# Constant-table matmuls ahead of the level scores, in the last recurrence of a two-block kernel

## The reference, cut to what matters

```
def step(state, inp):
    qi, ki, vi, gi = inp
    bcum = jnp.cumsum(gi, axis=2)
    o_inter = einsum('bhtk,bhkv->bhtv', qi * exp(bcum), state)
    rel = bcum[:, :, :, None, :] - bcum[:, :, None, :, :]
    decay = exp(where(incl, rel, -inf))
    scores = einsum('bhtk,bhsk,bhtsk->bhts', qi, ki, decay)
    o_intra = einsum('bhts,bhsv->bhtv', scores, vi)
    blast = bcum[:, :, -1:, :]
    state = state * exp(blast) + einsum('bhsk,bhsv->bhkv', ki * exp(blast - bcum), vi)
```

## Time and profile before

| | us |
|---|---|
| median of 3 runs | 3305.14 (3305.09 to 3307.75) |
| the profiled execution | 3311.11 |
| its span, first to last instruction | 3309.8 |
| TensorE matmuls busy | 3013.6 |
| VectorE busy | 1568.6 |
| ScalarE busy | 983.8 |
| GpSimd busy | 320.6 |
| mean granted TensorE clock (share of full speed) | 0.951 |

### The profile page before, as it was taken

The page is one execution under the profiler, slowest core; times in us unless marked ns, Lnnn a source line. Parts: engine busy times, 40 slices in busy tenths (PEclk is TensorE's granted clock), DMA queues, the critical chain, the costliest instruction groups (busy, mean ns, idle before and its releaser), DMA issues.

```text
span 3309.8 us, 44104 instructions
## 1 busy us (share of the span) xinstructions
PE 3013.6 (91%) x18434; PEld 2407.2 (73%) x18434; DVE 1568.6 (47%) x3075; ACT 983.8 (30%) x1912; POOL 320.6 (10%) x594
## 2 busy tenths in 40 slices
PE   7988889999999999888699999999999798699998
PEld 4657688889976666677557888888566587478886
DVE  3122544444443255776864424334625566655354
ACT  2011432223331155234233212211315344232222
POOL 0000000000000000543600000000100144200001
PEclk9999999999999999799799999999999799899999
DMA  5423241222122110222422121121011010222321
GB/s 180 152 93 128 83 123 42 55 60 75 58 96 102 51 32 1 80 71 79 148 101 83 45 77 64 51 77 64 39 45 33 16 33 20 90 90 77 115 83 71
DMA packets 227299, 246.62 MB, mean 75 GB/s; under 512 B 5552, under 2 KB 193052, under 8 KB 225564
## 3 DMA queue, kind: packets, MB, share of 16 engines
q1 hardware_dynamic: 227100, 243.79, 22.9%
HBM read 234.34 MB, written 9.44 MB: 74 GB/s over the span
## 4 chain that ended last, share of the span: by engine, by line
PE 56%; DVE 8%; ACT 4%; issue 1%; POOL 1%; DMA 1%; ACTq 0%; DVEq 0%; POOLq 0%
PE PS L1959 53%; PE PS L1963 2%; PE PS L2168 2%; ACT AR L174 1%; DVE AR L2687 1%; DVE AR L2678 1%; ACT L169 1%; DVE AR L2923 1%; POOL AR L2955 0%; DVE STAT L2859 0%; DVE EX L2910 0%; ACT EX L174 0%; DMA WR<-in_w_in 0%; DVE AC L2915 0%; ACT STAT L174 0%
## 5 line engine op out<-in xcount | busy, mean ns | idle before, releaser
L1959 PE MATMUL PS<-WR,HT 128*128 128x256 f32 (+2 forms) x2256 | 514.7, 387 | 11.0 <-ACT AR L174 5.4
L1959 PEld LDWEIGHTS PS<-WR,HT 128*128 128x128 f32 x2256 | 381.5, 199 | 120.2 <-issue 75.0
L1959 PE MATMUL PS<-HI,WC 128*128 128x512 f32 (+2 forms) x1600 | 428.2, 353 | 0.7 <-DVE WC L2904 0.7
L1959 PE MATMUL PS<-AR 128*64 128x64 f32 (+8 forms) x3756 | 320.6, 270 | 75.3 <-ACT AR L174 17.5
L1959 PE MATMUL PS<-HT,WR 128*128 128x256 f32 (+3 forms) x1136 | 357.3, 469 | 21.3 <-ACT EX L174 5.8
L174 ACT ACTIVATE AR<-PS 128x256 f32<-128x256 f32 (+3 forms) x389 | 166.1, 452 | 684.7 <-PE PS L1959 540.8
L1959 PEld LDWEIGHTS PS<-AR 128*64 128x64 f32 (+5 forms) x3756 | 276.8, 174 | 127.1 <-issue 48.7
L1959 PE MATMUL PS<-DW,DH 128*128 128x384 f32 (+1 forms) x1344 | 357.4, 348 | 0.9 <-DVE AR L2542 0.9
L1959 PEld LDWEIGHTS PS<-HI,WC 128*128 128x128 f32 x1600 | 284.1, 189 | 42.3 <-DVE WC L2904 1.1
L1959 PEld LDWEIGHTS PS<-HT,WR 128*128 128x128 f32 (+2 forms) x1136 | 214.6, 195 | 132.0 <-issue 91.3
L1959 PE MATMUL PS<-LO,WC 128*128 128x512 f32 (+2 forms) x800 | 282.6, 353 | 0.0
(11 more groups left out here) (297 smaller groups left out, 4142.3 us busy)
## 6 DMA issues: line engine op xcount, KB each, us to landing
WR<-in_w_ffn_in SPq DMA_DIRECT2D x40, 1024.0 KB, 7.6
WR<-in_w_in_b SPq DMA_DIRECT2D x51, 512.0 KB, 6.0
WR<-in_w_mod SPq DMA_DIRECT2D x12, 2048.0 KB, 8.1
WR<-in_w_mod SPq DMA_DIRECT2D x24, 1024.0 KB, 5.6
WR<-in_w_ffn_out SPq DMA_DIRECT2D x22, 1024.0 KB, 4.9
WR<-in_w_in SPq DMA_DIRECT2D x40, 512.0 KB, 4.1
WR<-in_w_out SPq DMA_DIRECT2D x8, 2048.0 KB, 9.3
WR<-in_w_in_a SPq DMA_DIRECT2D x8, 1024.0 KB, 5.2
```

The source lines that it names most:

```text
L1959: mm = lambda o, l, r, start, stop: e.o.matmul(o, l, r, start=start, stop=stop, skip_group_check=True)
```

## The change

Heads 2 and 3 of layer 1 get a mark `warm`. In `hl3` the wait for the unit's free banks moves ahead of the wait for its level weights, and for marked heads two matmuls stand between the two waits: the identity as stationary operand, the first 512 columns of the constant table as moving one, each into one bank of the unit's pair. The unit's own matmuls then start new sums in the same banks.

```
-        self.cum, ..., self.gneed = {}, {}, {}, False, False, False, None
+        self.warm, self.cum, ..., self.gneed = False, {}, {}, {}, False, False, False, None
...
+                H.warm = l == 1 and h > 1
...
             def hl3(n, H, i, d, L, until):
                 k, rev = H.dirs[d][0], H.dirs[d][2]
                 x3 = L["xb"][0:H.K, :].rearrange("p (l n) -> p l n", l=7)
+                e.wait_all(until)
+                for t in range(2 if H.warm else 0):
+                    mm(L["S"][:, t, :], ident, CON[:, 0:512], True, True)
                 e.wait_all(L["weighed"])
-                e.wait_all(until)
                 for t in range(2):
```

More of the change, by code:

```diff
@@ L247, in __init__ @@
         self.state, self.q_ready, self.steps, self.lv, self.am, self.slots = {}, {}, [], {}, {}, {}
-        self.cum, self.kt, self.dec, self.begun, self.multiplied, self.ended, self.gneed = {}, {}, {}, False, False, False, None
+        self.warm, self.cum, self.kt, self.dec, self.begun, self.multiplied, self.ended, self.gneed = False, {}, {}, {}, False, False, False, None
 def build(nc, A, out, dump=None):
```

## The result

The changed kernel takes 3321.95 us (median of 5 runs, 3317.20 to 3326.51) against 3305.86 for the kernel before on the same chip (3305.09 to 3307.75): ratio 1.0045, 95% interval 1.0034 to 1.0056. A second set of five runs gave 3318.77, ratio 1.0041 (1.0028 to 1.0053). So it is 12 to 16 us slower; 8.9 were forecast. Both sets are of five runs of one program, and their medians differ by 3.2 us.

A forecast was written before the change was run, and what follows sets the result against it. TensorE, busy 91% of the span, was taken as the bound wherever it does not idle. Terms 5.1 + 1.7 + 0.4 + 1.7 = 8.9 us on the 3305.14 median gave 3314.0, range 3308.5 to 3319.5.

The forecast's parts named there:

- head 2, units 0 to 2: Three pairs at full clock where TensorE does not idle: 3 x 1.71 = 5.1 us, all passed on.
- head 2, unit 3: Pair between transposes and unit: 0.7 of it at half clock, the rest and the unit at full clock; 1.7 us.
- head 3, unit 0 (units 1 and 2: 0): Unit 0's pair is mostly covered by 1.5 us free, leaving 0.4; units 1 and 2 are hidden in idle time.
- head 3, unit 3: Pair between a half-clock output and the unit whose end releases VectorE: 1.7 us if the clock runs as before.
- last output: Head 3's last output, at the recurrence's end: no change in the main case, half clock from 2856 on as before.
- the term for what lies behind the fence: After the recurrence: work starts from the shifted fence, so nothing takes the 8.9 us back; no further change counted.
- The slower rival of the prediction: Clock low more often, in heads 2 and 3: unit 3 of head 2 at 4.0, head 3 at 6.9; 3321, chance 0.07.
- my bounds of 0.5 and 4.0: Head 2's unit 3: 0.5 us with the clock up at once, 4.0 with the rise only behind the unit.
- the prediction's own sign of being wrong: Head 3: the prediction is wrong if the output before unit 3 runs at clock 1.00; 0.50 was expected.
- the clock stays up: Rival for head 3: it costs -0.3 instead of 2.1; 6.5 or 4.9 us in all, 3310 to 3311.6; chance 0.20.
- The rival's -0.7 for this piece: Head 3, unit 3: a full-clock output wins about 2.1, pays the pair, and VectorE is then the bound.
- My argument against the rival: Head 3: no pair stands in the gaps before 2844.94 and 2855.03; about 3 us idle remain ahead of the output.

The follow-up runs named there:

- swap_only: The two waits in the changed order with no matmul added, against the kernel before: 3305.83 us against 3306.54, ratio 0.9999.
- h3_gaps: Swapped waits and added pairs only before units 1 and 2 of head 3, against the kernel before: 3306.12 us against 3306.54, ratio 1.0001.
- tail: Pairs only before unit 3 of head 2 and units 0 and 3 of head 3, against the kernel before: 3309.97 us against 3305.35, ratio 1.0015.
- again: The changed kernel run and profiled once more, nothing altered, against the kernel before: 3318.77 us against 3306.54, ratio 1.0041.
- l0_first3: Three pairs before units 0 to 2 of head 2 in layer 0, none in layer 1, against the kernel before: 3313.21 us against 3305.35.
- after_fills: The changed kernel plus two constant-table matmuls for each of three idle times behind the recurrence: 3318.23 us, against 3305.35 for the kernel before.
- gapfill2: gapfill plus two matmuls in each of four later idle times, against the kernel before: 3299.48 us against 3306.00, ratio 0.9977.
- two_pairs: Pairs only before units 0 and 1 of head 2, against the kernel before: 3309.14 us against 3306.00, ratio 1.0011.
- one_pair: One pair only, before unit 0 of head 2, against the kernel before: 3312.90 us against 3306.00, ratio 1.0016.
- h2_first3: Pairs only before units 0 to 2 of head 2, against the kernel before: 3315.06 us against 3306.54, ratio 1.0026.
- gapfill: The kernel before with constant-table matmuls only in TensorE's idle times in heads 2 and 3, no pairs: 3307.28 us against 3305.35, ratio 1.0006.

## Why the prediction was wrong

The direction was right, the size was not: the median was 3321.95, and the range ended at 3319.5. The second set's median, 3318.77, would have been inside the range; the profiles, which agree with each other, put both at 14 us over before where 8.9 were forecast. By its own steps, the changed profile against the one before:

| step | forecast | measured |
|---|---|---|
| swap of the waits | 0 | 0 (swap_only) |
| head 2, units 0 to 2 | 5.1 | 5.5 |
| head 2, unit 3 | 1.7 | 2.5 |
| head 3, unit 0 (units 1 and 2: 0) | 0.4 | 1.3 |
| from VectorE's read to the output ahead of unit 3 | 0 | -0.2 |
| head 3, unit 3 | 1.7 | 0.15 |
| last output | 0 | -1.4 |
| end of the recurrence | 8.9 | 7.9 |
| behind it | 0 | 6.1 |

**The step that failed** is the term for what lies behind the fence, put at 0 in the one sentence "A fence follows, and what is behind it starts from there, so nothing takes it back." I had looked only for something that could take time back and priced the 460 us behind the fence at nothing. They held idle times of TensorE of about 2 us that the clock had survived. In the changed kernel it falls behind three of them, 4.9 us, and stays low longer in the output projection's first products, 1.2 us. The slower rival of the prediction came out near the measured time with 3321, but by luck: it put the low clock into heads 2 and 3, where the clock was in fact better than forecast.

**Head 2's first three pairs** were right in mechanism: no idle time ahead of them, the chain TensorE's, all of it passed on. 1.71 a pair was 0.1 too low each, since the step from the 512-column records to the unit's small ones costs something too. The price of the Trainium skill ("TensorE: Matmul & The Clock Gate", Back-to-back issue gap) is for a bf16 matmul; the f32 pair took 1.81 to 1.91 us, about four times the 0.43 by that price.

**Head 2's unit 3**: after the same 6.38 us idle the clock rose about 4.9 us behind TensorE's return (mean 0.63 over 6.7 us, so full for the last 1.7) where it had been 3.5 in before. So the whole pair, 3.55 us, ran at half clock, not 0.7 of it; 2.5 lies inside my bounds of 0.5 and 4.0, but I had copied one instance of the rise as if it were fixed.

**Head 3**: the row at 0.50 in 2829.9 to 2834.8 shows that output slower throughout, which put unit 0 at 1.3 (2.8 us more work, 1.5 of slack). Then the prediction's own sign of being wrong came true: the clock was 1.00 in the output ahead of unit 3. Its rival "the clock stays up" was right about that. The output took 2.7 us where it had taken 4.4, which paid the pair (0.15), and the last output gained 1.4. The rival's -0.7 for this piece was too good: it called VectorE the bound, but the piece still ends with TensorE, at 2.70 + 1.91 + 2.11 us. Its reason, that the longest gap is filled, does not hold either: h3_gaps filled it and had the fall in that output, tail left it empty and had none. My argument against the rival, that about 3 us of idleness are as long as gaps after which the clock was low, took falls seen elsewhere for a property of a gap's length. The two profiles contradict that: 2.29 us idle did no harm in before and brought a fall in the changed kernel.

What decides whether the clock falls in a given gap is settled only in part. It is reproducible as far as it was profiled (changed and again agree within 0.1 us in every stretch, and so do before, swap_only and l0_first3); it depends on how much was added before (one, two, three pairs: 5.9, 0, 4.2 us behind). Behind the last output no filled gap had a fall (two in after_fills, four in gapfill2), but 20 of the 34 times that one of the three later gaps stood empty it had none either.

One thing sorts all the profiles without fills behind the recurrence, though it is not an explanation. Where the clock fell inside head 3's last output (3.8 to 4.3 us: before, swap_only, l0_first3, h3_gaps, two_pairs, tail), none of the three later gaps brought a fall. Where that output ran at full clock throughout (2.79 us: the changed kernel and again, one_pair, h2_first3, gapfill), two or all three of them did. So the 1.4 us won in the last output and the 4.2 to 6.1 us lost behind it come together. Whether the one brings the other, or both follow from something earlier, no run here separates. A rule that gives the fall from the added time alone was not tried.

## What to carry to other kernels

Matmuls that keep TensorE's clock up must be shorter than the idle time in which they stand, and that has to be read unit by unit: here one unit of eight waited for its weights, and pairs put before all eight cost 14 us, where fills in real gaps, in the recurrence and behind it, gained 6.9. Fill the gaps on the whole path behind as well, and look at the granted clock up to the kernel's end: a gain of 5.9 us was given back entirely behind the recurrence, 4.9 us of it in three gaps of about 2 us. A change of a few us before such gaps can cost or save as much again there, so a small ablation should be compared stretch by stretch: one pair measured dearer than two.

## What the runs showed that was not expected

- The same idle time of TensorE (2.29 us, between the same instructions) left the clock at 1.00 in one program and was followed by 0.55 in another. Each such fall cost 1.5 to 1.7 us.
- The pattern of falls was the same in two executions of a program: between the two profiles of the changed kernel no stretch from head 1's last output to the end differed by more than 0.1 us, although that output started at 2760.67 in one and at 2758.08 in the other.
- Pairs added about 1240 us earlier left every later stretch unchanged within 0.1 us; the same pairs just ahead of the recurrence's end changed the last 445 us by 4.2.
- In eleven profiles without fills behind the recurrence, either the clock fell in the last output (six) or it fell behind two or three of the later gaps of about 2 us (five), never both and never neither.
